# Dealing the work beside six gather stages anew

## The chip, the cores and the metric

The kernel runs on one core of a Trainium2 chip. The metric is the device time of one execution in microseconds (us), as the median of several runs. A core has TensorE (PE, matrix products into PSUM), VectorE (DVE), ScalarE (ACT), GpSimd (POOL, which here issues the indirect DMAs) and SyncE (SP, which here issues the plain DMAs).

## The reference, cut to what matters

Two transformer blocks run one after the other over 512 tokens of width 1024. All of the change lies in the last layer of the second block, a product-key retrieval of single-neuron experts. For each of 512 tokens and 8 heads it picks 16 of 16384 experts, so 128 experts a token:

```
q = (xb @ w_query).reshape(TOKEN_BLOCK, P_HEADS, 2, P_HALF)
s = jnp.einsum('thpk,hpnk->thpn', q, sub_keys)
sv, si = lax.top_k(s, P_TOPK)                  # 16 of 128 keys in each half
fv, fpos = lax.top_k(cand, P_TOPK)             # 16 of their 256 sums
eidx = jnp.take_along_axis(cidx, fpos, axis=-1)
g = jax.nn.softmax(fv, axis=-1)
u = u_tab[eidx]
act = gelu(einsum('td,thkd->thk', xb, u))      # 128 dot products a token
out = einsum('thk,thkd->td', g * act, v_tab[eidx])
```

Each table has 16384 rows of 1024 floats (64 MB). "The first table" is `u_tab`, "the second" is `v_tab`.

## The kernel before, in words

The tokens are four blocks of 128, called t = 0 to 3; a partition is a token. The last layer runs as six stages, in this order: U0, V0, U1, V1, V2, V3.

**Gathers.** Each stage has 128 gathers. One gather is one indirect DMA issued by POOL (`gather`, the line 2700) that fetches 128 rows of 4 KB, one for each token of the block: 512 KB. Stage U0 gathers rows of the first table for block 0; VectorE forms a dot product with each (`dot`, line 2007). Stage V0 gathers rows of the second table for block 0; TensorE adds them up with weights (line 1178), four gathers a step, so a V stage has 32 steps, called m0 to m31. U1 and V1 do the same for block 1. V2 and V3 gather the second table for blocks 2 and 3. At the end of each V stage `finish(t)` on VectorE takes the sum.

**No U2 and U3.** For blocks 2 and 3 the dot products with the first table aren't made from gathered rows. The whole table is streamed in 128 plain DMAs of 512 KB by SP (line 2761, `raw<-ucols`), and TensorE multiplies each piece with the 256 tokens: this is one `dense` step (j = 0 to 127; 8 matrix products, line 1114). ScalarE moves the results of two dense steps at a time into the tile `Aj` (line 2546). Half of the table's scores, 64 dense steps, fill `Aj`. They are then picked over by 64 `ext` steps and two more that drain: TensorE copies key numbers to all partitions (line 1141), ScalarE makes a one-hot matrix of them (lines 2557 and 2559), TensorE chooses with it (`chosen`, line 1127), and VectorE picks and sums in one call for every four (lines 2055 to 2064). So dense 0 to 63 must end before ext 0, ext 0 to 65 before ScalarE may store dense 64 and later, dense 127 before ext 66, and ext 66 to 131 end the scores of blocks 2 and 3. Ext 99 ends block 2's and ext 131 block 3's.

**Ranking.** The choice of experts (the two `top_k`) for blocks 2, 3 and 1, in this order, is cut into 60 `topk` parts on VectorE; TensorE makes their key scores (`keys`, line 1075). Parts 40 to 49 are the first half of block 1. Their last one gives the row numbers (line 1953) for which POOL waits before the first gather of U1. `ids` steps turn row numbers over on TensorE (line 1097).

**Who does what when.** The dictionary `BESIDE` deals these works over the six stages. An entry (what, a, z, first, last) spreads the items a to z-1 evenly over the steps first to last of that stage (128 steps in a U stage, 32 in a V stage). Each engine's program is one fixed order made from it: a step's gather work, then its items. An engine waits in that order and passes nothing. In a U stage TensorE has only the items of the table, so it isn't tied to the gathers, only to VectorE by `keys` and `ids`. In a V stage its items stand between the weighted sums. ScalarE's `weights(1)`, at step 36 of U1, waits for the end of VectorE's ranking, with its stores of dense results behind it.

**Buffers.** Gathers go into a ring of slots of 4 KB a partition. POOL issues a gather when its slot is free. A list says at which gather (counted over all stages, 0 to 767) a slot joins the ring, because its memory is used by something else before: 9 slots from 0, one at 10, two each at 24, 128 and 200, four at 306, then the three slots in `raw`, which SP's plain loads of the first table use until then, and 16 slots in `Aj`. SP loads at most three pieces of the table ahead (`NU`). In U1 POOL also waits, before gather k, for the dense steps that the plan has at step k-8 (`BEHIND`):

```
if t and k >= BEHIND:
    for what, a, z in pace("U", t, k - BEHIND):
        if what == "dense" and z > a:
            G.wait_ge(*at["dn", z - 1])
```

Once, after load 100, SP writes block 0's finished rows out (`back(0)`) and waits for that before it goes on loading.

Of the kernel before, what the change touches and what calls it, by code (L numbers as in the profile page):

```python
# [37 lines left out]
for _n, _w in ROWS:  # L38
# [10 lines left out]
NU = 3  # L49
# [4 lines left out]


BESIDE = {
    ("U", 0): [("topk", 0, 22, 20, 124), ("ids", 0, 1, 12, 12), ("ids", 1, 2, 122, 122), ("dense", 0, 64, 0, 127)],
    ("V", 0): [("topk", 22, 40, 0, 14), ("topk", 40, 50, 15, 31), ("ids", 2, 3, 17, 17), ("ext", 0, 32, 1, 15),
               ("ext", 32, 66, 18, 31)],
    ("U", 1): [("topk", 50, 60, 0, 36), ("ids", 3, 4, 44, 44), ("dense", 64, 124, 0, 127)],  # L60
    ("V", 1): [("dense", 124, 128, 0, 2), ("ext", 66, 120, 3, 31)],
    ("V", 2): [("ext", 120, 132, 0, 6)],
    ("V", 3): [],
}

# [75 lines left out]
def build(nc, packs, rows, brows, x, meta, W, skT, ucols, utab, vtab, out):  # L141
    ctx = ExitStack()
    with ctx:
        def sb(name, n, dt=F32, p=128):
            return ctx.enter_context(nc.sbuf_tensor(name, [p, n], dt))
# [8 lines left out]
        raw = sb("raw", NP_RING * 8 * CW)  # L154
# [211 lines left out]
        Aj = sb("Aj", 256 * JC)  # L366
# [9 lines left out]
        for n, slots in ((0, [B2b[:, :], big2[:, 2048:3072], big2[:, 3072:4096], *(more[:, i * 1024:(i + 1) * 1024] for i in range(3)),  # L376
                              hres[:, 1024:2048], hres[:, 2048:3072], hres[:, 3072:4096]]),
                         (10, [raw[:, 3072:4096]]), (24, qslot(0)), (128, qslot(2)), (200, qslot(3)),
                         (306, [*qslot(1), skw[:, 0:1024], skw[:, 1024:2048]]),
                         (420, [raw[:, i * 1024:(i + 1) * 1024] for i in range(NU)]),  # L380
                         *((440 + 8 * i, [Aj[:, 1024 * i:1024 * (i + 1)]]) for i in range(16))):
            for g in slots:
                gs.append(g)
                comes.append(n)
# [3 lines left out]
        for n in range(len(STAGES) * NB):  # L388
            free = [i for i in range(NG) if comes[i] == n] + free
            i = free.pop(0)  # L390
# [2526 lines left out]
```

## Time and profile before

| | |
|---|---|
| median of 3 runs (lowest, highest) | 2275.85 us (2273.55, 2275.86) |
| the profiled execution | 2278.65 us, its span 2276.8 us |
| busy: PE, DVE, POOL, ACT | 88%, 57%, 39%, 28% of the span |
| first gather of U0 | at 1065 us |
| HBM read | 584.29 MB, of them 402.70 MB by POOL's gathers |
| mean TensorE clock granted | 0.939 of full speed |

The profile shows one execution. Its page gives the span in 40 equal slices (56.9 us each). The granted clock is TensorE's share of 2.4 GHz, which is either 1.2 or 2.4 GHz; a value between them is a mean. Timeline rows give the start, the duration, the engine and line, what is written from what, and in brackets how long the engine idled before and what released it. The six stages lie, by the first gather and the first product of each, about at 1065, 1356, 1531, 1777, 1940 and 2100 us.

### The profile page before, as it was taken

Reading aid. Unit: us, or ns where it says so; the run is one execution under the profiler, and the core shown is the slowest. Engines: PE = TensorE matmul, PEld = TensorE weight load, DVE = VectorE, ACT = ScalarE, POOL = GpSimd, SP = SyncE. Lnnn points to the kernel's source line nnn. Section 1 sums busy time; section 2 is a strip of 40 time slices with the busy share of each in tenths; the row PEclk is TensorE's granted clock in tenths of the full one; section 3 lists DMA queues with packets and bytes.
Section 4 is the critical chain, followed back from the end, with each engine's and each line's share of the span. In section 5 each row is a group of like instructions: output and inputs, shape, how many; then the busy total and the mean of one; then the engine's idle time right before and its main releaser. Section 6 shows DMA issues by size and latency. Waiting matters only on the chain.

```text
span 2276.8 us, 31483 instructions
## 1 busy us (share of the span) xinstructions
PE 1998.5 (88%) x12505; PEld 1542.0 (68%) x12505; DVE 1308.9 (57%) x2926; ACT 639.1 (28%) x1077; POOL 894.0 (39%) x821
## 2 busy tenths in 40 slices
PE   8999989999999999889999988899889888755554
PEld 8786879898898787688888865568778555311110
DVE  4865467767456556765979887779866134300000
ACT  4335332322245233432111124441111245300000
POOL 0510000000000000011557657767668777777773
PEclk9999999999999999899999999999999999877777
DMA  5111245444321311024899999989999999999997
GB/s 207 57 38 36 97 168 190 168 185 185 112 93 56 111 56 56 6 88 156 316 345 414 415 415 391 378 339 416 402 408 418 418 418 417 417 416 417 416 416 307
DMA packets 147058, 590.04 MB, mean 259 GB/s; under 512 B 16336, under 2 KB 16464, under 8 KB 134240
## 3 DMA queue, kind: packets, MB, share of 16 engines
q0 software_dynamic: 110592, 402.70, 44.3%
q1 hardware_dynamic: 35136, 178.80, 20.7%
q10 hardware_dynamic: 1184, 6.53, 0.8%
q8 instruction: 100, 1.64, 0.3%
q14 instruction: 46, 0.38, 0.0%
HBM read 584.29 MB, written 3.67 MB: 258 GB/s over the span
## 4 chain that ended last, share of the span: by engine, by line
PE 31%; POOL 13%; DMA 11%; DVE 8%; issue 6%; ACT 1%; DVEq 0%; POOLq 0%; SPq 0%; ACTq 0%
PE ps L1114 9%; POOL big L2700 5%; DMA raw<-ucols 5%; PE ps L572 5%; PE ps L574 4%; PE ps L573 4%; POOL Aj L2700 4%; PE ps L1178 3%; DMA big<-vtab,big 3%; PE ps L1127 2%; DVE cols L2007 2%; DMA Aj<-vtab,big 1%; DMA hres<-vtab,big 1%; POOL raw L2700 1%; POOL hres L2700 1%
## 5 line engine op out<-in xcount | busy, mean ns | idle before, releaser
L1114 PE MATMUL ps<-rowb,raw 128*128 128x256 f32 x2048 | 459.1, 384 | 20.0 <-DMA raw<-ucols 18.4
L1114 PEld LDWEIGHTS ps<-rowb,raw 128*128 128x128 f32 x2048 | 387.8, 192 | 88.6 <-DMA raw<-ucols 17.7
L2622 POOL TENSOR_TENSOR small<-small,cols 128x1 f32<-128x1 f32 (+3 forms) x33 | 29.0, 882 | 899.0 <-DVE small L1623 386.9
L1178 PE MATMUL ps<-big,cols 128*32 128x512 f32 x804 | 257.4, 715 | 42.2 <-DMA Aj<-vtab,big 19.6
L1178 PE MATMUL ps<-Aj,cols 128*32 128x512 f32 x484 | 197.2, 806 | 79.1 <-DMA big<-vtab,big 35.9
L2700 POOL DMA_INDIRECT big<-vtab,big x201 | 195.9, 975 | 73.8 <-issue 58.3
L2546 ACT ACTIVATE Aj<-ps 128x512 f32<-128x512 f32 x64 | 68.2, 1068 | 407.3 <-PE ps L1114 407.3
L572 PE MATMUL ps<-xhb,whb 128*128 128x512 f32 (+1 forms) x432 | 167.5, 388 | 5.9 <-ACT fbig L2401 3.0
L2700 POOL DMA_INDIRECT big<-utab,cols x112 | 144.6, 1291 | 60.3 <-issue 29.6
L573 PE MATMUL ps<-xhb,wlb 128*128 128x512 f32 (+1 forms) x432 | 164.3, 380 | 0.0
L574 PE MATMUL ps<-xlb,whb 128*128 128x512 f32 (+1 forms) x432 | 164.1, 380 | 0.0
L2007 DVE CUSTOM_DVE_ANT_0 cols<-big 128x1024 bf16<-128x1024 f32 x112 | 135.4, 1226 | 36.2 <-DMA big<-utab,cols 31.3
L2079 DVE TENSOR_TENSOR cols<-ps,g2b 128x512 f32<-128x512 f32 x8 | 5.2, 688 | 253.8 <-PE ps L1178 253.6
L1127 PE MATMUL ps<-Aj,Ir 128*128 128x64 f32 x1024 | 141.9, 284 | 10.1 <-DVE cols L2060 8.2
L572 PE MATMUL ps<-whb,ah 128*128 128x256 f32 x512 | 146.0, 285 | 0.8 <-DVE al L1657 0.8
L2154 ACT ACTIVATE whb<-raw 128x2048 fp32r<-128x2048 f32 x51 | 97.5, 1912 | 165.7 <-DMA raw<-ff 108.5
L573 PE MATMUL ps<-whb,al 128*128 128x256 f32 x512 | 143.9, 281 | 0.0
L574 PE MATMUL ps<-wlb,ah 128*128 128x256 f32 x512 | 143.8, 281 | 0.0
L2060 DVE TENSOR_TENSOR cols<-cols,ps 128x512 f32<-128x512 f32 x64 | 43.6, 688 | 171.7 <-PE ps L1127 171.7
L1222 DVE TENSOR_TENSOR wlb<-raw,whb 128x2048 fp32r<-128x2048 f32 x51 | 116.9, 2293 | 40.1 <-ACT whb L2154 37.0
L1127 PEld LDWEIGHTS ps<-Aj,Ir 128*128 128x128 f32 x1024 | 130.7, 200 | 12.8 <-issue 9.7
L2557 ACT ACTIVATE Ir<-ps,cols 128x512 f32<-128x512 f32 x128 | 87.0, 680 | 160.3 <-PE ps L1127 151.4
(398 smaller groups left out, 4838.6 us busy)
## 6 DMA issues: line engine op xcount, KB each, us to landing
raw<-ucols SPq DMA_DIRECT2D x128, 512.0 KB, 6.7
raw<-ff SPq DMA_DIRECT2D x32, 1024.0 KB, 4.9
raw<-w SPq DMA_DIRECT2D x24, 1024.0 KB, 4.8
raw<-ada SPq DMA_DIRECT2D x24, 1024.0 KB, 4.8
raw<-wo SPq DMA_DIRECT2D x8, 1024.0 KB, 4.8
raw<-wq SPq DMA_DIRECT2D x8, 1024.0 KB, 4.8
hres<-x SPq DMA_DIRECT2D x8, 512.0 KB, 5.5
out<-hres SPq DMA_DIRECT2D x7, 512.0 KB, 8.7
```

The lines of the kernel that those rows point to most:

```text
L572: e.matmul(o, lhsT=lh, rhs=rh, start=(k == 0), stop=False)
L573: e.matmul(o, lhsT=ll, rhs=rh, start=False, stop=False)
L574: ins = e.matmul(o, lhsT=lh, rhs=rl, start=False, stop=(k == n - 1))
L1114: ins = e.matmul(PS[b][:, c:c + 256], lhsT=un[j % NU][:, k, :], rhs=h2T[k // 4][:, k % 4, :], start=(k == 0), stop=(k == 7))
L1127: ins = e.matmul(PS[b][:, c:c + JC], lhsT=Ir[:, (g % 2) * 512 + q * 128:(g % 2) * 512 + (q + 1) * 128], rhs=Atd[:, 4 * g + q, :], start=Tr ...
L1178: ins = e.matmul(PS[hf][32 * j:32 * j + 32, :], lhsT=win[:, c0:c0 + 32], rhs=gs[i][:, hf * 512:(hf + 1) * 512], start=(m == 0), stop=(m == ...
L1222: e.tensor_tensor(lo, raw_of(n), hi.bitcast(F32), ALU.subtract).then_inc(*V.mark("lo", u))
L2007: e.tensor_tensor_reduce(out=junk[k % 3], in0=gs[i], in1=h2[:, t, :], scale=1.0, scalar=0.0, op0=ALU.mult, op1=ALU.add, accum_out=act[:, t ...
L2154: e.activation(hi, raw_of(n), ACT.Copy).then_inc(*A.mark("hi", u))
L2546: e.activation(Adt[:, jl:jl + 2, :], PS[2 + pair % 2][:, :].rearrange("p (j t) -> p j t", j=2), ACT.Copy).then_inc(*A.mark("dv", pair))
L2557: e.activation(one, PS[KEYS2[g % 2]][:, :], ACT.Abs, bias=pidx).then_inc(*A.mark("ex_a", r, g))
L2700: e.indirect_dma_start(gs[i], None, utab if st == "U" else vtab, bass.IndirectOffsetOnAxis(ap=idx, axis=0)).then_inc(sems[f"l_g{i}"], 16)
```

## The change

Only numbers move. Eight dense steps go from U0 to the first steps of V0, twelve ext steps from V0 to the first steps of U1, twelve dense steps from U1 to V1, sixteen ext steps from V1 to V2. The slots of the ring that come from `raw` and `Aj` join it later. All instructions stay, and so does the order of each kind.

| stage | dense before, after | ext before, after | gathers |
|---|---|---|---|
| U0 | 64, 56 | 0, 0 | 128 |
| V0 | 0, 8 | 66, 54 | 128 |
| U1 | 60, 48 | 0, 12 | 128 |
| V1 | 4, 16 | 54, 38 | 128 |
| V2 | 0, 0 | 12, 28 | 128 |
| V3 | 0, 0 | 0, 0 | 128 |

```
 BESIDE = {
-    ("U", 0): [("topk", 0, 22, 20, 124), ("ids", 0, 1, 12, 12), ("ids", 1, 2, 122, 122), ("dense", 0, 64, 0, 127)],
-    ("V", 0): [("topk", 22, 40, 0, 14), ("topk", 40, 50, 15, 31), ("ids", 2, 3, 17, 17), ("ext", 0, 32, 1, 15),
-               ("ext", 32, 66, 18, 31)],
-    ("U", 1): [("topk", 50, 60, 0, 36), ("ids", 3, 4, 44, 44), ("dense", 64, 124, 0, 127)],
-    ("V", 1): [("dense", 124, 128, 0, 2), ("ext", 66, 120, 3, 31)],
-    ("V", 2): [("ext", 120, 132, 0, 6)],
+    ("U", 0): [("topk", 0, 22, 20, 124), ("ids", 0, 1, 12, 12), ("ids", 1, 2, 122, 122), ("dense", 0, 56, 0, 127)],
+    ("V", 0): [("dense", 56, 64, 0, 4), ("topk", 22, 40, 0, 14), ("topk", 40, 50, 15, 31), ("ids", 2, 3, 17, 17),
+               ("ext", 0, 26, 5, 17), ("ext", 26, 54, 18, 31)],
+    ("U", 1): [("ext", 54, 66, 0, 11), ("topk", 50, 60, 0, 36), ("ids", 3, 4, 44, 44), ("dense", 64, 112, 12, 127)],
+    ("V", 1): [("dense", 112, 128, 0, 8), ("ext", 66, 104, 9, 30)],
+    ("V", 2): [("ext", 104, 132, 0, 18)],
     ("V", 3): [],
 }
```

```
-                         (420, [raw[:, i * 1024:(i + 1) * 1024] for i in range(NU)]),
-                         *((440 + 8 * i, [Aj[:, 1024 * i:1024 * (i + 1)]]) for i in range(16))):
+                         (444, [raw[:, i * 1024:(i + 1) * 1024] for i in range(NU)]),
+                         *((460 + 10 * i, [Aj[:, 1024 * i:1024 * (i + 1)]]) for i in range(16))):
```

## Rows read from the trace of the kernel before

**Rows 1.** Page: GB/s in 40 slices, the gathers' queue, the table's loads

```profile
GB/s 207 57 38 36 97 168 190 168 185 185 112 93 56 111 56 56 6 88 156 316 345 414 415 415 391 378 339 416 402 408 418 418 418 417 417 416 417 416 416 307
...
q0 software_dynamic: 110592, 402.70, 44.3%
...
raw<-ucols SPq DMA_DIRECT2D x128, 512.0 KB, 6.7
```

**Rows 2.** Stretches: us, busy PE, PEld, DVE, ACT, POOL, clock, DMA share, GB/s

```profile
1065.00:1180.00 115.00, 113.38 (x523) 95.60 (x521) 96.03 (x311) 19.37 (x21) 60.35 (x49) 1.00 0.87 312
1180.00:1349.00 169.00, 163.35 (x756) 139.80 (x756) 153.91 (x420) 25.26 (x25) 113.94 (x94) 1.00 1.03 415
...
1380.00:1513.00 133.00, 121.00 (x1053) 79.01 (x1053) 102.15 (x357) 68.40 (x119) 97.54 (x97) 0.94 1.00 388
1513.00:1536.00 23.00, 19.74 (x130) 14.14 (x130) 16.70 (x22) 7.58 (x12) 10.70 (x11) 0.85 0.65 232
1536.00:1606.00 70.00, 66.78 (x308) 56.82 (x306) 66.50 (x196) 8.55 (x8) 52.33 (x44) 1.00 1.03 417
1606.00:1628.00 22.00, 18.04 (x68) 15.07 (x69) 20.41 (x40) 3.62 (x5) 8.70 (x7) 0.77 1.00 384
...
1689.00:1772.00 83.00, 77.60 (x354) 66.00 (x352) 53.18 (x88) 14.19 (x14) 63.01 (x48) 1.00 1.02 411
1772.00:1960.00 188.00, 158.93 (x1345) 97.45 (x1345) 60.64 (x97) 79.61 (x142) 142.85 (x149) 0.95 1.03 418
```

**Rows 3.** Timeline: VectorE held in U0 by ScalarE's exponentials

```profile
1144.86 0.29 DVE L1993 TENSOR_REDUCE small<-cols 128x8 f32<-128x128 f32 x1 [6.04 <-ACT cols L2529]
```

**Rows 4.** Groups of TensorE, 1100 to 1340 us: the dense products

```profile
L1114 PE MATMUL ps<-rowb,raw 128*128 128x256 f32 x975 | 216.3, 381 | 6.1 <-DMA raw<-ucols 6.0
```

**Rows 5.** Timeline: last dot of U0, last store, first product of V0

```profile
1346.34 1.22 DVE L2007 CUSTOM_DVE_ANT_0 cols<-B2b,big 128x1024 bf16<-128x1024 f32 x1
...
1351.70 1.02 ACT L2546 ACTIVATE Aj<-ps 128x512 f32<-128x512 f32 x1 [5.83 <-PE ps L1114]
...
1355.89 1.07 PE L1178 MATMUL ps<-big,cols 128*32 128x512 f32 x2 [0.69 <-ACT cols L2591]
```

**Rows 6.** Timeline: first product of steps m5, m14, m16, m18, m30 of V0

```profile
1380.04 0.62 PE L1178 MATMUL ps<-big,cols 128*32 128x512 f32 x2 [0.26 <-DMA more<-vtab,big]
...
1431.61 0.62 PE L1178 MATMUL ps<-big,cols 128*32 128x512 f32 x2
...
1448.40 1.07 PE L1178 MATMUL ps<-more,cols 128*32 128x512 f32 x2
...
1455.86 0.62 PE L1178 MATMUL ps<-big,cols 128*32 128x512 f32 x2
...
1515.23 0.62 PE L1178 MATMUL ps<-big,cols 128*32 128x512 f32 x2
```

**Rows 7.** Groups of TensorE, 1460 to 1515 us: the ext products

```profile
L1127 PE MATMUL ps<-Aj,Ir 128*128 128x64 f32 x217 | 29.0, 276 | 0.8 <-ACT Ir L2559 0.8
...
L1141 PE MATMUL ps<-big,small 128*128 128x128 bf16 x108 | 10.5, 220 | 0.0
```

**Rows 8.** The chain that ended last: the 16 weighted products of one step

```profile
1460.12 1.85 PE ps L1178 x16
```

**Rows 9.** Timeline: first and last of one ext call on VectorE

```profile
1519.06 1.29 DVE L2055 TENSOR_TENSOR cols<-cols,big 128x512 f32<-128x512 f32 x2
...
1521.46 1.27 DVE L2064 TENSOR_REDUCE big<-cols 128x8 f32<-128x512 f32 x2
```

**Rows 10.** Timeline of POOL: U1's first gather, and gather 52

```profile
1523.50 1.27 POOL L2700 DMA_INDIRECT more<-utab,cols  x1 [9.48 <-DVE cols L1953]
...
1617.44 1.33 POOL L2700 DMA_INDIRECT big<-utab,cols  x1 [11.04 <-PE ps L1114]
```

**Rows 11.** Timeline: TensorE held at step 44 of U1, first product of V1

```profile
1608.65 0.47 PE L1097 MATMUL ps<-cols 128*128 128x128 f32 x1 [4.70 <-DVE cols L1953]
...
1777.37 1.07 PE L1178 MATMUL ps<-more,cols 128*32 128x512 f32 x2 [4.41 <-DMA big<-vtab,big]
```

## The prediction

> **What bounds the kernel now.** I read the page first. From slice 20 on the DMA engines move 316 to 418 GB/s, and from slice 30 to the last but one they stay at 416 to 418 [rows 1]. The change touches nothing ahead of 1065 us, so the question is what bounds the 1212 us behind it. I call 512 KB, one gather or one load of the table, a unit. At 418 GB/s it takes 524288 / 418000 = 1.254 us. The 768 gathers and 128 loads are 896 units, 1124 us, of 1212. The engines are therefore a transfer pump with holes, and the time can only change by the size of the holes, wherever the work of TensorE stands.
>
> Then I cut the stretch into pieces whose rates differ [rows 2]. A piece of length L at rate g loses L x (1 - g/418). The start of U0 (1065 to 1180) loses 29 us, the rest of U0 1 us. V0 loses 9.5 us (1380 to 1513), the passage to U1 10.2 us (1513 to 1536), U1 0.2 us until 1606, 1.8 us until 1628 and about 1.8 us behind that. V1 loses nothing, and V2 and V3 run at 416 to 418 [rows 1]. I must ask of each hole what it becomes.
>
> **Start of U0.** Here too few slots are in flight, and VectorE has the ranking beside its dots (96 of 115 us busy). One part of this hole hangs on the change. VectorE waits 6.04 us for the exponentials of block 0 [rows 3], which stand at step 16 in ScalarE's order, behind the stores of the dense steps planned before it. These were dense 0 to 7, and are now 0 to 6, of which only 0 to 5 are stored by then. The wait shrinks by up to two dense steps, so it goes. One dense step costs 216.3 / (975/16) = 3.55 us [rows 4]. I take 5 us off this hole, between 0 and 7.
>
> **End of U0.** The DMA engines are full (415) and must carry 8 units fewer: 10.0 us earlier. TensorE has 28.4 us less to do. Before, it was the last: VectorE ended its last dot at 1347.6, but the last store of dense results came at 1351.7 to 1352.7, and the first product of V0 at 1355.9 [rows 5]. TensorE's lateness goes with its eight steps. What comes last next is VectorE, at 1347.6 less 10 from the units, and less 0 to 5 from the first hole: I take 1336. VectorE itself, 154 of 169 us busy [rows 2], doesn't allow much more. In U1, where TensorE isn't late, the first product of V1 comes 5.5 us behind the last dot, when its rows land [rows 11]. So m0 of V0 comes at 1341.5, 14.4 us earlier.
>
> **V0.** Steps m0 to m4 now have 8 dense steps, 1.6 each: 5.7 us, and with the weighted products (1.85 us [rows 8]) and the keys some 7.9 us a step, against (4 + 1.6) x 1.254 = 7.0 us of transfers. m5 comes at 1381, as late as before (1380.0 [rows 6]). From there I follow the old intervals. m5 to m14 took 51.6 us, 6.4 over the 45.2 of its 36 gathers: a decoding of the ranking held VectorE, behind it the ext call, behind that TensorE. Now ext starts only at m5 and this decoding has nothing behind it; at 5.0 us a step (four units) m14 comes at 1426. m14 to m16 took 16.8 us, with the second such stall, and is kept: 1443. m16 and m17 had no ext and took 7.5 us; now they have two each and take 10: 1453. m18 to m30 took 59.4 us with 29 ext steps, now 24. An ext costs TensorE 1.07 us for line 1127 and up to 0.39 for line 1141 [rows 7], so TensorE needs 52 to 54 us and the transfers 60; rows landed during the stall serve part of it: 57, m30 at 1510. Before it was 1515.2. With two instead of three ext steps at the end, V0 ends some 7 us earlier than before (1531); I take 8, and 4 to 15 as bounds. The lower one is TensorE gaining nothing by the thinner ext, the upper one TensorE's own sum without the transfers. By all this the holes of V0 and of the passage (9.5 and 10.2 us) shrink to some 2 and 6 us.
>
> **The first 44 steps of U1: the price.** This is the stretch where VectorE sets the pace (66.5 of 70 us busy at 417 GB/s [rows 2]), with dots, half a ranking and `finish(0)`. POOL issued U1's first gather at 1523.5 and was stopped before gather 52 until 1617.4, a wait for a dense step [rows 10]. TensorE was itself stopped at step 44, by the end of the ranking on VectorE [rows 11], and ScalarE's stores stood still behind the same event. Until that moment it had done the dense steps planned ahead of step 44, 64 to 83: 20 of them, each freeing one load. So in these 93.9 us 52 + 20 = 72 units were asked for, 90 us. The stretch was just balanced.
>
> Now ext 54 to 65 stand in front. VectorE gets three more ext calls, 3.7 us each from the start of the first group of one to the end of its last (1519.06 to 1522.73 [rows 9]): 11.0 us more ahead of the end of the ranking, which it reaches at step 36. Nothing hides them, since VectorE has no idle time here. And fewer dense steps are planned ahead of step 44: 48 x 32/116 = 13, of which TensorE can finish 12 (64 to 75; the next needs a store that stands behind ScalarE's `weights(1)`). POOL's rule stops it before gather 51. So 51 + 12 = 63 units are asked for, 79 us, in 93.9 + 11.0 = 105 us. This hole is 26 us against 4 before. Behind TensorE at step 44 are queued the dense steps, behind these the loads of SP and by the `BEHIND` rule the gathers, and VectorE then waits for them.
>
> POOL resumes at 1617.4 - 8 + 11 = 1620.4, 3 us later than before, with 9 units more still to carry: 9 x 1.254 = 11.3 us. The sum so far is +14.3 us.
>
> The Trainium skill ("DMA: Bandwidth & Descriptors", Specifications) gives the HBM limit of one core as about 358 GB/s. The trace disagrees: 418 over 188 us. By the page a unit would take an estimated 1.46 us, the nine units 13.2 us, and the forecast would be 2 us higher.
>
> **Rest of U1.** Behind 1620 there are 77 gathers and 36 loads, 142 us of transfers, against 36 dense steps, 128 us of TensorE. Before it was 145 against 142, closely tied, and SP's `back(0)` made a hole of about 1 us. TensorE has room now: I take 1 us off, between 0 and 3.
>
> **V1.** Nine steps with 16 dense: 1.78 x 3.55 + 1.85 = 8.2 us each, against 5.78 x 1.254 = 7.2 us of transfers. The ring has 20 slots when V1 begins, 25 us of transfers; the first product comes about 5.5 us behind the last dot, so some 18 us are left. Nine steps eat 9 us of them, and a slow clock at the start 2 or 3 more. The reserve holds, at no cost. If it did not, the price is up to 9 us. Behind m9 a step has 1.73 ext, about 4.3 us of TensorE, under the 5.0 of four units. The later slots of `raw` and `Aj` cost nothing: V1 before ran at 418 GB/s, and 20 slots are more than its latency needs; the `Aj` slots are asked for no earlier than ext frees them.
>
> **V2, V3.** 1.5 ext a step in m0 to m18, 4.1 us against 5.0. Block 2's scores end with ext 99, at m28 of V1, in time; block 3's at m18 of V2. No change.
>
> **Sum.** -8 + 11 + 11.3 - 1 = +13.3, say +14 us against the profiled execution (span 2276.8, time 2278.65). This one lies 2.8 us above the median of the runs shown. The forecast is 2275.85 + 14 = 2290 us, +0.6%.
>
> **Rivals.** (a) V0 ends so early that it pays for all. Its two holes and the one at the start of U0 hold 29 + 9.5 + 10.2 us. Everything behind is fixed by the three terms +11, +11.3, -1, so the end of V0 must come 21.3 us earlier to break even, and each us beyond is won. For it speaks that TensorE was the bound from 1065 to 1513 (PE 91 to 99% busy) and has 12 ext less by then. Against it: five new steps of 7.9 us, one stall kept, and the transfer floor of 5.0 us a step. At 26 us earlier the time is 2271. Chance 0.10. (b) The same in part, the end of V0 16 to 25 us earlier, or the start of U1 less tight because VectorE's calls fall into waits: within 0.2% (4.6 us, about what a measurement of this kernel can tell from no change), 2277. Chance 0.14. (c) As forecast up to V1, and V1's reserve runs dry, because the ring begins with less than 20 slots in flight: +9 us, 2299. For it speaks that TensorE is idle ahead of V1 and starts at the slow clock. Chance 0.14. (d) The forecast, 2282 to 2296: 0.62.
>
> The bounds: E, the end of V0, by 4 to 15 us earlier; the ext calls 9 to 12; the units 10 to 12.5; back(0) 0 to -3; V1 0 to 9. That makes +2 to +27; with the tails cut to 2 in 10 it is 2278 to 2301. Faster by over 0.2%: 0.10. Within: 0.14. Slower: 0.76.
>
> **What would show it.** The first product of V0 at 1338 to 1345; no stall between m5 and m14; V0 over at 1516 to 1527. Then, the heart of it, 70 to 90 us behind that a stretch in which the DMA engines move 280 to 340 GB/s where they moved 417, VectorE 95% busy, TensorE idle 15 to 20 us ahead of its step 44, POOL stopped before gather 51 until 1615 to 1627. V1 at 418 GB/s with steps of 8 us. The prediction is wrong if this stretch stays near 417, or if V0 ends ahead of 1510.

## The result: 1.2% slower, twice the forecast

The changed kernel took 2304.07 us in the median of 4 runs (2302.65 to 2305.94), the kernel before 2275.86 us. The ratio is 1.0119, with a 95% interval of 1.0106 to 1.0133. In a second set of runs (a1 below) it was 1.0100 (1.0083 to 1.0117). The sign was forecast. The size, +28 us against +14, lies outside the range, which ended at 2301. The profiled execution has a span of 2300.8 us, 24.0 more than before.

The page of the changed kernel, the GB/s in 40 slices (57.5 us each), against [rows 1]:

```profile
GB/s 202 59 37 36 99 172 191 161 175 187 108 91 74 92 56 56 19 92 170 312 390 415 415 340 384 404 328 348 368 418 418 419 402 416 413 413 415 417 416 329
```

Slices 23, 27 and 28 (counted from 0) are new holes; slice 26 had one before too (339). The stretches of the changed kernel, with the columns of [rows 2]:

```profile
1067.00:1182.00 115.00, 110.63 (x508) 92.75 (x506) 99.44 (x330) 19.43 (x21) 62.15 (x51) 1.00 0.86 315
1182.00:1340.00 158.00, 130.66 (x607) 111.59 (x605) 144.33 (x391) 19.43 (x19) 109.32 (x86) 0.93 1.03 415
1340.00:1400.00 60.00, 55.69 (x278) 39.67 (x282) 29.32 (x129) 8.55 (x13) 27.61 (x27) 0.90 0.90 330
1400.00:1522.00 122.00, 111.26 (x1014) 72.71 (x1006) 85.34 (x310) 64.61 (x114) 92.13 (x94) 0.97 1.01 402
1522.00:1545.00 23.00, 14.40 (x138) 10.83 (x137) 21.88 (x36) 11.80 (x19) 10.53 (x10) 0.97 0.63 230
1545.00:1577.00 32.00, 27.69 (x130) 25.89 (x131) 30.91 (x90) 8.97 (x13) 16.78 (x17) 0.60 0.77 283
1577.00:1620.00 43.00, 34.44 (x156) 28.81 (x154) 41.06 (x114) 3.19 (x3) 34.05 (x27) 0.94 1.02 406
1620.00:1650.00 30.00, 25.59 (x107) 21.83 (x108) 27.75 (x52) 5.35 (x6) 15.18 (x11) 0.85 0.87 322
...
1780.00:1960.00 180.00, 163.44 (x1193) 104.85 (x1193) 36.61 (x60) 57.63 (x100) 113.83 (x120) 0.96 1.02 413
1960.00:2286.00 326.00, 198.39 (x1344) 69.46 (x1348) 39.69 (x61) 40.81 (x88) 242.82 (x254) 0.82 1.03 415
```

By L x (1 - g/418) the holes are now: start of U0 28 us (before 29); V0 12.6 + 4.7 = 17.3 (before 9.5); the passage to U1 and U1 10.3 + 10.3 + 1.2 + 6.9 = 28.7 (before 10.2 + 0.2 + 1.8 + 1.8 = 14.0); V1 2.2 (before 0). Together that is about 24 us more. The span behind U0's first gather grew by 21.7 us, so the sum of the listed holes is right to about 2 us: the pieces not listed and the rounding of the rates make up the rest. The pump-with-holes reading stands, and the question is only which holes grew. The distances from U0's first gather (1065.47 before, 1067.81 after) say where:

| event, us behind U0's first gather | before | after | shift | forecast |
|---|---|---|---|---|
| last dot of U0 ends | 282.1 | 279.4 | -2.7 | -11.6 |
| first product of V0 | 290.4 | 290.0 | -0.4 | -14.4 |
| first product of m5 | 314.6 | 331.5 | +16.9 | +1 |
| first gather of U1 | 458.0 | 464.3 | +6.2 | -8 |
| POOL goes on behind U1's step 44 | 552.0 | 562.5 | +10.5 | +3 |
| end of the span | 1211.3 | 1233.0 | +21.7 | +13 |

The whole spans differ by 24.0 us; the other 2.3 us stand ahead of U0, where the kernels are the same. One profile is one execution, and such distances vary from one to the next. The nine profiles with U0 as before (before, e2, e4, e6, e8, e13, e14, e16, e17) have V0's first product 290.4 to 294.0 us behind U0's first gather, and the six with U0 as in the changed kernel (after, a1, e3, e5, e9, e15) have it at 287.5 to 293.3. So it is no accident of one profile that the forecast -14.4 didn't come, while a shift of 1 to 3 us would not be seen. The timeline of the changed kernel at the places of [rows 3], [rows 5], [rows 6], [rows 10] and [rows 11]:

```profile
1143.49 0.29 DVE L1993 TENSOR_REDUCE small<-cols 128x8 f32<-128x128 f32 x1 [2.39 <-ACT cols L2529]
...
1337.83 0.45 PE L1097 MATMUL ps<-cols 128*128 128x128 f32 x1 [22.69 <-DVE big L1892]
...
1340.13 0.29 DVE L2035 CAST big<-ps 128x128 uint32<-128x128 f32 x1
...
1340.56 0.45 PE L1097 MATMUL ps<-cols 128*128 128x128 f32 x1 [2.28 <-DVE big L2035]
1340.80 12.83 PE L1114 MATMUL ps<-rowb,raw 128*128 128x256 f32 x48
...
1346.03 1.22 DVE L2007 CUSTOM_DVE_ANT_0 cols<-B2b,big 128x1024 bf16<-128x1024 f32 x1
...
1353.66 1.02 ACT L2546 ACTIVATE Aj<-ps 128x512 f32<-128x512 f32 x1 [5.85 <-PE ps L1114]
...
1357.86 1.07 PE L1178 MATMUL ps<-big,cols 128*32 128x512 f32 x2 [0.69 <-ACT cols L2591]
...
1399.32 0.62 PE L1178 MATMUL ps<-big,cols 128*32 128x512 f32 x2
...
1532.07 1.27 POOL L2700 DMA_INDIRECT more<-utab,cols  x1 [10.03 <-DVE cols L1953]
...
1572.42 1.97 POOL L2700 DMA_INDIRECT big<-utab,cols  x1 [10.52 <-PE ps L1114]
...
1624.02 6.04 PE L1114 MATMUL ps<-rowb,raw 128*128 128x256 f32 x16 [11.93 <-ACT Aj L2546]
...
1630.33 0.94 POOL L2700 DMA_INDIRECT big<-utab,cols  x1 [11.57 <-PE ps L1114]
```

At the end of U0 TensorE waits for VectorE at step 122 (`ids`, 1340.56, released by line 2035), and the three dense steps behind that are again the last. In the kernel before, this place looks so:

```profile
1341.00 0.30 PE L1097 MATMUL ps<-cols 128*128 128x128 f32 x1 [0.47 <-DVE big L2035]
1341.14 10.53 PE L1114 MATMUL ps<-rowb,raw 128*128 128x256 f32 x48
```

Step 122 comes 275.5 us behind U0's first gather before and 272.8 after, 2.8 us earlier, as VectorE does. But before, TensorE arrived there in time with VectorE, while now it had stood idle for 22.69 us, and then for 2.28 more. Its three dense steps took 12.83 us instead of 10.53: the granted clock was 0.50 from 1340.6 to 1345.0, the lower of the two levels (1.2 GHz), where it was 1.00 before. (In a1 it was 0.50 as well, behind an idle time of 24.06 us.) That ate 2.3 of the 2.8 us.

The DMA engines had meanwhile run through their queue. The median time from issue to landing, between 1300 and 1360 us, from the DMA view of each kernel; first before:

```profile
raw<-ucols SPq DMA_DIRECT2D x14, 512.0 KB, 6.8
big<-vtab,big POOLq DMA_INDIRECT x7, 19.6
...
more<-vtab,big POOLq DMA_INDIRECT x3, 19.8
```

and after:

```profile
raw<-ucols SPq DMA_DIRECT2D x8, 512.0 KB, 6.7
big<-vtab,big POOLq DMA_INDIRECT x6, 7.5
...
more<-vtab,big POOLq DMA_INDIRECT x3, 7.1
```

V0's first gathers took 19.6 us to land before and take 7.5 us now. Six loads fewer were asked for in these 60 us. The queue of 12 us more had carried the DMA engines over the passage from U0 to V0. Without it they run dry from 1340 on.

### The profile page after: what moved, and what is told of

Read it like the earlier page. It is cut to its first block, busy times and chain, and to the rows that moved or that the text cites. A ratio compares the mean times of both kernels' runs of the same rounds, so it can differ in the third digit from the quotient of the medians.

```text
span 2300.8 us, 31473 instructions
## 1 busy us (share of the span) xinstructions
PE 1993.1 (87%) x12505; PEld 1546.7 (67%) x12505; DVE 1313.5 (57%) x2926; ACT 638.0 (28%) x1077; POOL 892.2 (39%) x821
## 3 DMA queue, kind: packets, MB, share of 16 engines
q1 hardware_dynamic: 35136, 178.80, 20.6%
## 4 chain that ended last, share of the span: by engine, by line
PE 25%; POOL 17%; DVE 14%; issue 8%; DMA 6%; ACT 1%; DVEq 0%; POOLq 0%; ACTq 0%
POOL big L2700 7%; DVE cols L2007 6%; PE ps L1114 5%; PE ps L572 4%; PE ps L573 4%; PE ps L574 4%; POOL Aj L2700 4%; PE ps L1178 3%; DMA big<-vtab,big 2%; POOL more L2700 2%; POOL hres L2700 2%; POOL raw L2700 2%; PE ps L1127 1%; DMA more<-utab,cols 1%; PE ps L963 1%
## 5 line engine op out<-in xcount | busy, mean ns | idle before, releaser
L1114 PE MATMUL ps<-rowb,raw 128*128 128x256 f32 x2048 | 465.8, 387 | 26.3 <-DMA raw<-ucols 13.9
L2622 POOL TENSOR_TENSOR small<-small,cols 128x1 f32<-128x1 f32 (+3 forms) x33 | 28.7, 873 | 893.0 <-DVE small L1623 386.9
L1178 PE MATMUL ps<-big,cols 128*32 128x512 f32 x840 | 222.8, 678 | 49.0 <-DMA big<-vtab,big 20.9
L2700 POOL DMA_INDIRECT big<-vtab,big x210 | 204.6, 974 | 101.8 <-issue 60.3
L1178 PE MATMUL ps<-Aj,cols 128*32 128x512 f32 x428 | 160.6, 768 | 55.9 <-DMA Aj<-vtab,big 23.0
L1178 PE MATMUL ps<-more,cols 128*32 128x512 f32 x252 | 113.1, 693 | 17.8 <-DMA big<-vtab,big 8.2
```

The source lines that it names most:

```text
L1114: ins = e.matmul(PS[b][:, c:c + 256], lhsT=un[j % NU][:, k, :], rhs=h2T[k // 4][:, k % 4, :], start=(k == 0), stop=(k == 7))
L1178: ins = e.matmul(PS[hf][32 * j:32 * j + 32, :], lhsT=win[:, c0:c0 + 32], rhs=gs[i][:, hf * 512:(hf + 1) * 512], start=(m == 0), stop=(m == ...
L2700: e.indirect_dma_start(gs[i], None, utab if st == "U" else vtab, bass.IndirectOffsetOnAxis(ap=idx, axis=0)).then_inc(sems[f"l_g{i}"], 16)
```

## The experiments

In the edits below only the entries of `BESIDE` that differ are shown. The chips differ in what they move in the V stages: on one kind V2 and V3 run at about 416 GB/s and the kernel before takes 2276 to 2278 us; on the other at 358 to 370 GB/s (2000 to 2300 us), where it took 2376 and 2389 us in two sets. So only ratios to the kernel before, run on the same chip, are compared, and the sets on the faster chips decide the sizes. A gain or loss with a sign is the ratio times the time before; the difference of the medians can be 1 or 2 us away from it.

**e1, e7: no dense behind step 122 of U0.**

```
-("U", 0): [..., ("dense", 0, 56, 0, 127)]          # on the changed kernel
+("U", 0): [..., ("dense", 0, 56, 0, 121)]
```

> The changed kernel with one edit: the 56 dense steps of U0 are spread over steps 0 to 121 instead of 0 to 127, so that none stands in TensorE's order behind the ids of step 122, for which it waits on VectorE. Theory (VectorE sets the end of U0, and the three dense steps left behind its step 122, 10.7 us and a store, come last): V0's first product comes 6 to 9 us earlier, and the time falls from 2304 to 2295 to 2299. Rival (the end of U0 hangs on transfers or on VectorE's own last dots): no change, 2303 to 2305.

> The kernel of e1 again (the 56 dense steps of U0 over steps 0 to 121), now beside the changed kernel on one chip. Theory: 5 to 9 us less than the changed kernel. Rival: no difference.

e1 fell on a slower chip: 1.0101 (1.0084 to 1.0118). In e7 the kernel took 2298.67 us (1.0088, 1.0071 to 1.0105) beside 2300.85 for the changed kernel (a1). V0's first product came 287.0 us behind U0's first gather instead of 290.0 in a1, and the later events 2.5 to 3.5 us earlier too. Both intervals overlap, so the time doesn't settle it, and 3 us is within what profiles of one plan differ by; 287.0 (286.9 in e1) is just below all fifteen profiles named above. The 3 us are a balance of two larger terms. From the end of the last dot to the first product it took 10.1 us in a1 and 1.9 in e7, so the three dense steps behind step 122 did cost 8.2 us, within the 6 to 9 expected. But the last dot itself ended 5.2 us later (285.1 against 279.9): the same 56 steps stand closer together now, and VectorE waited 8.1 us for key scores behind them (line 1876; 4.6 in a1) and 5.0 for the exponentials (2.4).

> The changed kernel itself, to stand on the same chip as the runs beside it. If this chip moves about 418 GB/s, 2300 to 2308; if it moves about 370 GB/s as in the runs e1 to e4, 2390 to 2410.

**e2, e8, e16: the move out of U0 undone.**

```
-("U", 0): [..., ("dense", 0, 56, 0, 127)]          # on the changed kernel
-("V", 0): [("dense", 56, 64, 0, 4), ..., ("ext", 0, 26, 5, 17), ...]
+("U", 0): [..., ("dense", 0, 64, 0, 127)]
+("V", 0): [..., ("ext", 0, 26, 1, 17), ...]
```

> The changed kernel with only the first part undone: 64 dense steps in U0, none in V0, ext 0 to 25 from step 1 on; U1, V1, V2 and the ring stay changed. Theory (the eight dense steps ran at no cost beside VectorE's U0, and cost TensorE and transfer time in V0): V0 begins as before at about 1356, its hole falls from 17 us to 2 to 6 because TensorE has 12 ext less there, and the time is 2288 to 2294. Rival (as the prediction had it, the move out of U0 brings U0 forward by 10 us and the loss is all in U1): undoing it makes the kernel slower than the changed one, 2306 to 2316.

> The kernel of e2 again (the changed kernel with 64 dense steps in U0, none in V0), on another chip if it comes so. In e2, on a chip with slower transfers, it stood 0.8% above before. Theory (half of the loss is the move out of U0, half is U1): V0's first product at the same distance from U0's first gather as before (290 us), U1's first gather 8 to 13 us earlier than in the changed kernel, and a time of 10 to 14 us above before. Rival (the loss is all in U1): 22 us or more above before.

> The kernel of e2 once more (the changed kernel with 64 dense steps in U0 and none in V0, which is also the kernel before with the edits of e13 and e14 together). Theory (the parts add up): 4.6 + 7 = 11 us above before, 9 to 15 us, on a chip of 418 GB/s. Rival (the two parts of U1 compound): 18 us or more above before.

On slower chips it was 1.0081 (1.0053 to 1.0109) and 1.0085 (1.0056 to 1.0113), on a faster one 2289.43 us beside 2277.28: 1.0058 (1.0043 to 1.0073). Set against the changed kernel's two ratios, 1.0100 and 1.0119, undoing the move gives back 0.4 to 0.6% on the faster chips, 10 to 14 us. The two kernels did not stand in one set there. In e16 U1's first gather came 452.1 us behind U0's, 12.2 earlier than in the changed kernel.

**e3, e9, e15: the move out of U0 alone, on the kernel before.**

```
-("U", 0): [..., ("dense", 0, 64, 0, 127)]
-("V", 0): [..., ("ext", 0, 32, 1, 15), ...]
+("U", 0): [..., ("dense", 0, 56, 0, 127)]
+("V", 0): [("dense", 56, 64, 0, 4), ..., ("ext", 0, 32, 5, 17), ...]
```

> The kernel before with only the first part done: 56 dense steps in U0, 8 in V0's steps 0 to 4, ext 0 to 65 all in V0 from step 5 on; U1, V1, V2 and the ring as before. Theory: U0 doesn't end earlier, V0 gets 28 us more of TensorE work in a stage that TensorE bounds, of which a few us come back by one stall less; 2292 to 2302. Rival (prediction): U0 ends 10 us and V0 begins 14 us earlier, 2270 to 2280.

> The kernel of e3 again (the kernel before with only the move of eight dense steps from U0 to V0). Theory: first product of V0 at 290 us behind U0's first gather, as before, and V0 longer by 12 to 20 us, which the time shows in full: 12 to 20 us above before. Rival (the step of the prediction that failed in the profile of the changed kernel fails only beside its other edits): 0 to 5 us below before.

> The kernel of e3 once more (only the move of eight dense steps from U0 to V0), because in e9, on a chip that moved less than 418 GB/s, it lay 0.6% above before and in e3 0.9%. Theory: 12 to 20 us above before. Rival: at or below before.

Slower chips gave 1.0086 (1.0067 to 1.0106) and 1.0058 (1.0036 to 1.0080), a faster one 2298.03 us beside 2278.20: 1.0080 (1.0062 to 1.0098), +18 us (19.8 between the medians). POOL in e15:

```profile
1546.26 1.26 POOL L2700 DMA_INDIRECT more<-utab,cols  x1 [14.81 <-DVE cols L1953]
```

Its first gather of U0 is at 1067.63, so U1 begins at 478.6, 20.6 us later than before. V0's first product is at 293.3, 2.9 later, which is within the spread of profiles; the other 17.7 us are lost in V0. V0 keeps its 66 ext steps here and has 28 us of dense steps ahead of them.

**e12: 32 dense steps left in U0.**

```
-("U", 0): [..., ("dense", 0, 56, 0, 127)]          # on the changed kernel
-("V", 0): [("dense", 56, 64, 0, 4), ..., ("ext", 0, 26, 5, 17), ("ext", 26, 54, 18, 31)]
+("U", 0): [..., ("dense", 0, 32, 0, 121)]
+("V", 0): [("dense", 32, 64, 0, 12), ..., ("ext", 0, 10, 13, 17), ("ext", 10, 54, 18, 31)]
```

> The changed kernel with only 32 dense steps in U0 (steps 0 to 121) and 32 in V0's steps 0 to 12, ext 0 to 9 in steps 13 to 17 and 10 to 53 behind; one look, for U0 alone, since V0 must become long. Theory (VectorE sets U0): with 24 units and 85 us of TensorE's work less than in the changed kernel, V0's first product still comes 275 to 290 us behind U0's first gather. Rival (transfers set it, as predicted): 30 us earlier, 255 to 262.

One run, 2354.53 us, as it had to be long. Its stretch to the end of U0, VectorE's row at the end, and the first product:

```profile
1180.00:1340.00 160.00, 82.24 (x343) 67.13 (x347) 151.28 (x413) 13.01 (x16) 114.24 (x90) 0.75 0.97 370
```

```profile
1334.41 1.22 DVE L2007 CUSTOM_DVE_ANT_0 cols<-B2b,big 128x1024 bf16<-128x1024 f32 x1
...
1337.52 1.07 PE L1178 MATMUL ps<-big,cols 128*32 128x512 f32 x2 [0.69 <-ACT cols L2591]
```

TensorE is busy for 82 of 160 us, the DMA engines move 370 GB/s, and VectorE is busy for 151. With U0's first gather at 1065.22 the last dot ends at 270.4 us and the first product comes at 272.3. That is below the 275 to 290 of the theory and far above the 255 to 262 of the rival. With 24 units (30 us) less, VectorE's end moved by 9.0 us against the changed kernel, and it can hardly move further, since it is busy (95%). VectorE's waits, listed from U0's first gather on, say where the 9 us come from: 6.8 us for landing rows and 4.6 for key scores behind dense steps are gone, and the wait for the exponentials is 2.6 longer (5.4 against 2.8). So the transfers were worth at most these 6.8 us of U0's length, and taking out the first eight units had not freed them (5.6 before, 6.8 in the changed kernel). The other 8.7 us lie behind the last dot: no dense step stands behind step 122 any more, and ScalarE loads its table while VectorE still works.

**e4: the ring's list alone.**

```
-(420, [raw[:, ...]]), *((440 + 8 * i, [Aj[:, ...]]) ...)     # on the kernel before
+(444, [raw[:, ...]]), *((460 + 10 * i, [Aj[:, ...]]) ...)
```

> The kernel before with only the ring's list changed (the slots of raw join at 444 instead of 420, those of Aj at 460 + 10i instead of 440 + 8i). Theory: no cost, 2274 to 2278, since V1 to V3 have 20 slots or more in flight and stay at 416 to 418 GB/s. Rival: V1 and V2 lose rate for want of slots, 2280 to 2290.

2372.13 us beside 2375.73 on a slower chip, 0.998 (0.9963 to 0.9998). It costs nothing there; on a faster chip it ran only together with the edit of e13.

**e13: dense from U1 to V1 and ext from V1 to V2 alone.**

```
-("U", 1): [..., ("dense", 64, 124, 0, 127)]        # on the kernel before; the ring as in e4
-("V", 1): [("dense", 124, 128, 0, 2), ("ext", 66, 120, 3, 31)]
-("V", 2): [("ext", 120, 132, 0, 6)]
+("U", 1): [..., ("dense", 64, 112, 0, 127)]
+("V", 1): [("dense", 112, 128, 0, 8), ("ext", 66, 104, 9, 30)]
+("V", 2): [("ext", 104, 132, 0, 18)]
```

> The kernel before with only the last parts of the change: U1 has 48 dense steps (64 to 111, steps 0 to 127), V1 16 dense and 38 ext, V2 28 ext, and the ring's new list; U0 and V0 as before, no ext in U1. Theory (units not asked for while VectorE ranks cost their transfer time): 16 instead of 20 dense steps are planned ahead of U1's step 44, so the hole there grows by about 4 units, and the time by 4 to 7 us, against before. Rival 1 (only the longer VectorE work costs anything): 0 to 2 us. Rival 2 (V1's sixteen dense steps in nine steps make V1 bound by TensorE): 10 us or more.

2283.04 us beside 2278.20: 1.0020 (1.0011 to 1.0030), +4.6 us, within the 4 to 7 expected. The stretch around step 44 of U1 has the hole:

```profile
1540.00:1600.00 60.00, 52.68 (x233) 44.45 (x231) 56.89 (x188) 6.41 (x6) 47.07 (x38) 0.94 1.03 416
1600.00:1630.00 30.00, 18.44 (x70) 15.49 (x71) 28.20 (x45) 3.98 (x5) 14.74 (x13) 0.72 0.87 331
```

331 GB/s over 30 us is a hole of 6.2 us, against 2.3 before (386 GB/s). V1 with its sixteen dense steps ran at 409 GB/s instead of 418 (1780 to 1960 us), a hole of 3.9 us more: not the 10 us or more of the second rival, but not nothing. The profile shown is of the slowest execution (2286.98 us), and the median doesn't say how the 4.6 us split between the two places.

**e14: ext 54 to 65 from V0 to U1 alone.**

```
-("V", 0): [..., ("ext", 0, 32, 1, 15), ("ext", 32, 66, 18, 31)]      # on the kernel before
-("U", 1): [..., ("dense", 64, 124, 0, 127)]
+("V", 0): [..., ("ext", 0, 26, 1, 17), ("ext", 26, 54, 18, 31)]
+("U", 1): [("ext", 54, 66, 0, 11), ..., ("dense", 64, 124, 12, 127)]
```

> The kernel before with only ext 54 to 65 moved from V0 to U1's steps 0 to 11, and U1's 60 dense steps in steps 12 to 127. Theory: V0 ends 8 to 13 us earlier with less work for TensorE, the stretch from U1's first gather to the end of POOL's stop before gather 52 grows by 9 to 12 us with VectorE's three more calls and by 3 to 4 units asked for later; the time is 0 to 6 us above before. Rival (V0's earlier end is the larger): 3 to 8 us below before.

2285.73 us beside 2278.20: 1.0031 (1.0020 to 1.0043), +7 us. The time lies 1 us above the 0 to 6 expected, and both terms were smaller than expected. U1's first gather came at 453.1, 4.9 us earlier than before (5.9 in e16, which has the same U0 and V0), not 8 to 13: the relief of V0 is real, and small. The stretch from there to the end of the ranking (line 1953) grew from 84.9 us to 90.2, not by 9 to 12.

**e5: more dense ahead of step 44.**

```
-("U", 1): [..., ("dense", 64, 112, 12, 127)]       # on the changed kernel
+("U", 1): [..., ("dense", 64, 80, 12, 43), ("dense", 80, 112, 45, 127)]
```

> The changed kernel with one edit: U1 has 16 of its 48 dense steps in steps 12 to 43 and 32 in steps 45 to 127, instead of 13 and 35. Theory (the hole of U1 is one of transfers not asked for, because few dense steps are planned ahead of step 44 and POOL's rule stops with them): 3 units more are asked for ahead of the end of the ranking, so 3 to 5 us less than the changed kernel. Rival (the hole is the time that VectorE needs for 12 more ext): no change.

2295.42 us beside 2300.85 for the changed kernel in the same set: ratios to before of 1.0074 (1.0051 to 1.0096) and 1.0100 (1.0083 to 1.0117). The stretches of e5:

```profile
1545.00:1577.00 32.00, 27.30 (x133) 25.77 (x134) 30.87 (x90) 8.96 (x13) 16.29 (x17) 0.64 0.78 290
1577.00:1620.00 43.00, 42.57 (x197) 36.38 (x196) 41.05 (x116) 5.33 (x5) 28.68 (x26) 1.00 1.02 408
1620.00:1650.00 30.00, 28.61 (x132) 24.32 (x131) 27.75 (x52) 5.53 (x6) 22.96 (x19) 1.00 1.03 417
```

The hole behind step 44 is gone (417 GB/s where the changed kernel has 322, 6.9 us), the one at 1545 to 1577 is not. The intervals of the two times overlap, so the time alone doesn't show the gain. The events do: from U1's first gather to the end of the span it is 762.1 us in e5, 770.5 in a1 and 768.7 in the changed kernel's first profile, 6.6 to 8.4 less, about the size of the closed hole.

**e6, e10, e11, e17: attempts to beat the kernel before.**

```
e6:  ("topk", 40, 50, 15, 31)     ->  ("topk", 40, 50, 15, 27)                               # V0
e10: ("dense", 0, 64, 0, 127)     ->  ("dense", 0, 8, 0, 23), ("dense", 8, 64, 24, 127)      # U0
e11: ("dense", 0, 64, 0, 127)     ->  ("dense", 0, 8, 0, 23), ("dense", 8, 60, 24, 121)      # U0
     ("ext", 0, 32, 1, 15)        ->  ("dense", 60, 64, 0, 2), ("ext", 0, 32, 3, 17)         # V0
e17: ("dense", 64, 124, 0, 127)   ->  ("dense", 64, 87, 0, 43), ("dense", 87, 124, 45, 127)  # U1
```

> The kernel before with one edit: parts 40 to 49 of the ranking are spread over steps 15 to 27 of V0 instead of 15 to 31, so that the row numbers of block 1 are there four steps before V0 ends. Theory (the hole at the passage from V0 to U1, 10.2 us, comes from POOL waiting for these numbers): POOL's wait of 9.5 us goes, and the time falls by 5 to 9 us against the kernel before. Rival (VectorE only stalls TensorE elsewhere in V0): within 2 us of before.

> The kernel before with one edit: 8 of the 64 dense steps of U0 in steps 0 to 23 and 56 in steps 24 to 127, instead of an even spread (12 and 52). Theory (VectorE sets the pace of U0, and two of its waits, 6.0 us for the exponentials behind ScalarE's stores and 4.6 us for the keys at step 24 behind TensorE's dense steps, hang on how many dense steps stand in front): VectorE's last dot comes 6 to 9 us earlier, but TensorE, with the same 64 steps, is then the last, and the time is 0 to 4 us less than before. Rival (VectorE's waits move to a later place): no change within 1 us.

> The kernel before with the light start of e10, 60 dense steps in U0, none behind its step 121, and the other four in steps 0 to 2 of V0, ext from step 3 on. Theory: with TensorE relieved of four steps the earlier end of VectorE's U0 is used, V0's first product comes 6 to 10 us earlier, V0 gets 14 us more of TensorE's work, and the time is between 5 us less and 5 us more than before. Rival (anything moved into V0 costs its TensorE time): 8 us or more above before.

> The kernel before with one edit: U1 has 23 of its 60 dense steps in steps 0 to 43 and 37 in steps 45 to 127, instead of 21 and 39. Theory (the hole behind step 44 is of transfers not asked for while TensorE waits there): 1 to 3 us less than before, if ScalarE's stores let TensorE do them. Rival (the stores stand behind the exponentials of block 1, and the time doesn't move): within 1 us.

e6: 1.0004 (0.9995 to 1.0014). The wait for the row numbers went, and POOL then stood at another place, by the `BEHIND` rule, for a dense step of U1 that TensorE can't begin before V0 ends:

```profile
1537.12 1.66 POOL L2700 DMA_INDIRECT raw<-utab,cols  x1 [7.76 <-PE ps L1114]
```

So the expected gain of 5 to 9 us did not come: with the numbers early, the passage hangs on the end of V0 on TensorE. e10, on a slower chip: 1.0038 (1.0016 to 1.0061), slower, where 0 to 4 us less was expected. Its first product of V0 came 299.9 us behind U0's first gather, where the profiles with 64 even steps on the slower chips (e2, e4, e8) have 291.2 to 292.9, because TensorE's 64 steps were pushed back; and the two waits of VectorE that it was to shorten did not shrink (6.8 and 5.7 us, against 5.8 and 4.6 in e4). e11: 1.0015 (0.9987 to 1.0043), no difference shown. e17: 2275.42 us beside 2277.28, 0.9993 (0.9984 to 1.0002); the hole behind step 44 closed (418 GB/s from 1600 to 1630 us where the kernel before has 386), but the 1.9 us between the medians aren't clear of the noise. None beats the kernel before.

## Why the prediction was right in its sign and wrong in its size

**The frame held.** The sum of the holes explains the growth of the span to about 2 us. From the moment when POOL goes on behind step 44 to the end it is 659.4 us before and 670.5 after: 11.1 us, against the forecast 11.3 for nine units, less 1 for `back(0)`.

**The step that failed: "The DMA engines are full (415) and must carry 8 units fewer: 10.0 us earlier", and with it "TensorE's lateness goes with its eight steps".** The DMA engines were full in U0, and still did not set its end. VectorE did. It was busy for 154 of 169 us [rows 2], and I had read this as a limit on how much more could be gained, where it was the bound itself. Of its idle time in that stretch, the waits for landing rows make about 6 us. The full DMA engines were filled by a queue: TensorE ran through its dense steps as fast as it could, each asked for the next load, and the gathers beside them took 16 to 20 us to land, in a ring that allowed it. Eight units fewer shortened the queue, not the stage. e12, one execution, shows it by taking out 24 more units: VectorE's last dot came 9 us earlier, not 30, and only 6.8 of its waits were for rows. The first product of V0 moved by -0.4 us instead of -14.4. VectorE's last dot gave 2.7 us, a part of the 3.65 by which its wait for the exponentials had shrunk (6.04 to 2.39 us, where I took 5 off; in e5 and e15, with the same U0, it was still 5.0). The three dense steps behind step 122, which both kernels have, lost 2.3 of that to the lower clock. That TensorE's lateness would go with its eight steps had overlooked that the steps go from all over U0, while the last three still stand behind a wait for VectorE.

**What followed from it.** I had priced V0's first five steps at 7.9 us each of TensorE; they took 8.3. But I set their start 14 us too early, and let them begin on a reserve of gathers in flight. The reserve was the very queue that the eight loads had made. V0's first gathers landed in 7.5 us instead of 19.6, and then the DMA engines stood dry behind a stage that TensorE paces. That is the 12.6 us from 1340 to 1400. Later V0 made good 10.7 us of the 16.9 lost by m5, by fewer ext and one stall less, about as reckoned. (TensorE's need between m18 and m30, 24 ext of 1.07 to 1.46 us and 12 times 1.85, is 48 to 57 us, not 52 to 54; the 57 us taken came true, 56.9.) In sum U1 began 14.2 us later than forecast. That is the whole error of the forecast span and more. Made alone, the move costs 18 us (e15); undone in the changed kernel it gives back 10 to 14 (e16 against the changed kernel's two ratios).

**U1: the mechanism right, two sizes off.** I had the stretch from U1's first gather to POOL's going on at 93.9 us before and 105 after; it took 98.3. VectorE did get its 11 us: from its first dot to the end of the ranking it was 71.1 us before (1537.3 to 1608.4) and 82.2 after (1539.8 to 1622.0). But its first dot came only 7.7 us behind U1's first gather, where it had been 13.8: V0's thinner end let VectorE begin sooner, which I had left out (8.0 us in e14 with the thinner V0, 13.8 in e13 with the old one). POOL was stopped before gather 51, as forecast. A stop before gather 22 (10.5 us, 1572.4) was not: the first dense step of U1 falls on step 14, behind TensorE's ext, and the `BEHIND` rule holds gather 22 for it. TensorE waited 9.8 us there for VectorE's picking (line 2060), and behind the longest of these waits, 7.2 us, it ran from 1546 to 1566 at a granted clock of 0.50, the lower level. The stop makes the hole of 10.3 us at 1545 to 1577; e14 and e5 have the same stop (10.3 us each). In holes, passage and U1 make 28.7 us where I had 6 + 26.

**V1 and the ring near the forecast.** V1 lost 2 us on its sixteen dense steps, where I had taken none and allowed up to 9; alone, in e13, it lost 3.9. The ring's list cost nothing in e4, on a slower chip.

**The rivals.** (a) and (b) needed V0 to end 16 to 26 us earlier; it ended later. (c), V1 running dry, gave 2 of its 9 us. The case that came, a U0 that isn't bound by transfers, was not among them. The stretches gave its condition: VectorE 91% busy.

**The range and the signs.** The bounds were added up wrongly: -15 + 9 + 10 - 3 + 0 is +1, and -4 + 12 + 12.5 - 0 + 9 is +29.5, not +2 and +27. The measured +28 would lie inside the wider sum, but that would have been luck, since the term that failed, the end of V0, came 6.2 us later where the bounds had it 4 to 15 earlier. Of the signs, the first product of V0 (1357.9, not 1338 to 1345) showed the failure. The stretch of low rate in U1 came as forecast (322 GB/s from 1620 to 1650 us), with TensorE idle 11.9 us ahead of it instead of 15 to 20 and POOL stopped until 1630 instead of 1615 to 1627.

**The parts.** On the faster chips: dense U0 to V0 +0.80% (e15), ext V0 to U1 +0.31% (e14), dense U1 to V1 with ext V1 to V2 +0.20% (e13). The last two together are e16, +0.58% against a sum of 0.51. All three sum to 1.31% against the measured 1.19 and 1.00%. With these intervals the parts may simply add up; that ext moved out of V0 relieves the stage that got the eight dense steps would make the whole smaller than the sum, but no run shows it clear of the noise. Each of the three is a loss by itself, so none pays for another.

## What to carry to other kernels

A DMA meter at its ceiling doesn't say that the stage is bound by transfers. Look at how long a transfer takes to land: here gathers took 16 to 20 us, and 7.5 when eight loads were taken away, and the stage ended when it did before. Requests were running ahead of their user. Such a queue may be what bridges the next passage, where the buffers aren't refilled. When work is dealt over stages, look for the stage whose bound engine doesn't do it: the eight dense steps were nearly free in U0, where VectorE was the bound, and cost 18 us in V0, where TensorE was. And count how many requests are planned ahead of each wait.

## What the runs showed of the hardware that was not expected

The same kernel took longer on some chips than on others, and only some stages did: the kernel before took 2276 to 2278 us in four sets and 2376 and 2389 us in two. In V2 and V3 (2000 to 2200 us) the slower chips moved 356 to 364 GB/s where the faster ones moved 416. But in U0 (1180 to 1340 us) they moved 414 or 415 GB/s, the same as the faster ones, and at the end of U1 (1760 to 1780 us) 417 or 418. Two rows of e9:

```profile
1180.00:1340.00 160.00, 134.30 (x617) 114.34 (x616) 147.34 (x391) 20.45 (x21) 107.92 (x87) 0.94 1.03 414
...
2000.00:2300.00 300.00, 195.67 (x1063) 67.28 (x1064) 32.05 (x49) 30.61 (x66) 195.92 (x205) 0.77 0.94 359
```

So it isn't that everything a slower chip transfers is slow: the stages that gather from the second table are, and those that gather from and stream the first one aren't. Why, no run here shows.

The Trainium skill ("DMA: Bandwidth & Descriptors", Specifications) puts a core's HBM limit at about 358 GB/s, as half of what it gives for a stack that two cores share. The V stages on the slower chips lie near it. U0 and the end of U1 on the same chips don't (414 to 418), nor do V2 and V3 on the faster ones (about 416). No run here records whether a neighbouring core was at work.
